# Joints and merge steps in another order, and the rotary exchange of rows by small DMAs instead of a matmul

## The reference

```python
x = layer_norm(ALPHA * x + 0.5 * swiglu_1(x))
xp, q, k, v, xq, gates = split(x @ w_in)      # pool input, attention, cross query, 3 gates of 1024
q, k = rope_partial(q), rope_partial(k)       # first 16 of 64 dims of a head: x1*cos - x2*sin, x2*cos + x1*sin
merged = (sigmoid(g0) * (pool(xp) @ w_br_pool) + sigmoid(g1) * (window_attention(q, k, v) @ w_br_swa)
          + sigmoid(g2) * (cross_attention(xq, mem) @ w_br_cross))
x = layer_norm(ALPHA * x + merged @ w_o)
x = layer_norm(ALPHA * x + 0.5 * swiglu_2(x))  # swiglu: (silu(x @ w_gate) * (x @ w_up)) @ w_down
```

## Time and profile before

| | us |
|---|---|
| median of 3 runs (lowest, highest) | 2549.53 (2546.69, 2554.24) |
| profiled execution | 2552.91 |
| its span, first to last instruction | 2551.1 |
| TensorE busy | 2442.1 (96%) |
| VectorE, ScalarE, GpSimd busy | 64%, 48%, 24% |
| mean granted TensorE clock | 0.982 |

### The profile page before, as it was taken

One profiled execution on the slowest core, in us unless ns is written; L12 is line 12 of the kernel. 1 busy time (PEld: TensorE's weight loads), 2 busy tenths in 40 slices (PEclk: granted clock), 3 DMA queues, 4 the chain that ended last, 5 costly groups with the idle time before them and its releaser, 6 DMA issues.

```text
span 2551.1 us, 45264 instructions
## 1 busy us (share of the span) xinstructions
PE 2442.1 (96%) x17684; PEld 2374.3 (93%) x17684; DVE 1631.7 (64%) x2716; ACT 1221.1 (48%) x2459; POOL 615.6 (24%) x544
## 2 busy tenths in 40 slices
PE   6999999999999999999999999989999999999997
PEld 6999999899999889999989999979999998999996
DVE  2878776435444587777687777664443447878775
ACT  4555555334422365655465556542342225655653
POOL 1333333120000123333323333321100002333332
PEclk9999999989999999999999999989999999999999
DMA  6132223222122212232213222222112222222221
GB/s 222 63 120 83 100 88 122 67 75 56 51 82 75 83 67 100 75 106 86 100 50 110 91 100 88 105 90 94 43 55 75 75 75 83 71 96 100 81 103 54
DMA packets 53523, 220.63 MB, mean 86 GB/s; under 512 B 15520, under 2 KB 18464, under 8 KB 40224
## 3 DMA queue, kind: packets, MB, share of 16 engines
q1 hardware_dynamic: 53312, 217.74, 25.1%
HBM read 213.64 MB, written 6.04 MB: 86 GB/s over the span
## 4 chain that ended last, share of the span: by engine, by line
PE 78%; DVE 12%; ACT 5%; DVEq 2%; issue 2%; DMA 0%; POOL 0%; ACTq 0%
PE pair L1796 12%; PE pair L1798 11%; PE pair L1797 11%; PE pair L1648 9%; PE pair L1650 9%; PE pair L1652 9%; PE S L1734 2%; DVE htl L1104 2%; PE S L1796 2%; PE S L1798 2%; PE S L1797 2%; ACT hth L660 1%; PE S L1890 1%; DVE TP L1024 1%; PE TP L1950 1%
## 5 line engine op out<-in xcount | busy, mean ns | idle before, releaser
L1796 PE MATMUL pair<-xth,hiA 128*128 128x288 f32 x1216 | 358.9, 295 | 13.9 <-ACT c L712 7.8
L1797 PE MATMUL pair<-xtl,hiA 128*128 128x288 f32 x1216 | 358.8, 295 | 0.0
L1798 PE MATMUL pair<-xth,loA 128*128 128x288 f32 x1216 | 358.4, 295 | 0.0
L612 ACT ACTIVATE hiA<-TP 128x512 fp32r<-128x512 f32 (+1 forms) x372 | 194.0, 555 | 220.0 <-DVE TP L1029 136.0
L1562 POOL TENSOR_TENSOR loB<-rawB,hiB 128x512 fp32r<-128x512 f32 (+1 forms) x128 | 159.5, 1247 | 480.2 <-ACT hiB L612 480.2
L1010 DVE TENSOR_TENSOR loA<-rawA,hiA 128x1024 fp32r<-128x1024 f32 x108 | 133.9, 1240 | 218.7 <-ACT hiA L599 218.3
L1648 PE MATMUL pair<-xh,hiA 128*128 128x288 f32 x1088 | 253.8, 310 | 18.9 <-DVE loA L1010 9.0
L1015 DVE TENSOR_TENSOR loA<-TP,hiA 128x512 fp32r<-128x512 f32 (+1 forms) x372 | 236.3, 635 | 31.7 <-ACT hiA L612 29.0
L1650 PE MATMUL pair<-xl,hiA 128*128 128x288 f32 x1088 | 243.0, 300 | 0.0
L1652 PE MATMUL pair<-xh,loA 128*128 128x288 f32 x1088 | 242.7, 300 | 0.0
L1796 PEld LDWEIGHTS pair<-xth,hiA 128*128 128x128 f32 x1216 | 228.0, 187 | 15.4 <-issue 15.3
(11 more groups left out here) (322 smaller groups left out, 7001.2 us busy)
## 6 DMA issues: line engine op xcount, KB each, us to landing
rawA<-in_wblk SPq DMA_DIRECT2D x108, 512.0 KB, 3.5
rawB<-in_wg SPq DMA_DIRECT2D x44, 1024.0 KB, 4.8
rawA<-in_wg SPq DMA_DIRECT2D x44, 1024.0 KB, 4.8
rawB<-in_wd SPq DMA_DIRECT2D x24, 768.0 KB, 4.2
rawA<-in_wd SPq DMA_DIRECT2D x24, 768.0 KB, 4.4
rawA<-in_wt_d SPq DMA_DIRECT2D x4, 1024.0 KB, 4.7
rawB<-in_wt_d SPq DMA_DIRECT2D x4, 1024.0 KB, 4.8
mcs<-in_mks SPq DMA_DIRECT2D x2, 2048.0 KB, 10.0
```

The costliest lines, as they stand in the source:

```text
L612: nc.scalar.activation(slot((hiA, hiB), prod, n), src, ACT.Copy).then_inc(f_hi, 1)
L1796: nc.tensor.matmul(bank, wt_hi, xt[0], start=start, stop=False, skip_group_check=True)
L1797: nc.tensor.matmul(bank, wt_hi, xt[1], start=False, stop=False, skip_group_check=True)
L1798: last = nc.tensor.matmul(bank, wt_lo, xt[0], start=False, stop=i == n - 1, skip_group_check=True)
```

## The change

Six places. (1) Memory stage: odd pairs are rounded to buffers of their own (`mwh`, `mwl`), x is rounded after the first pair, and the waits of `round_w` follow. (2) The head of the FFN: other orders on ScalarE and VectorE; `u2` of unit 3 is copied right after P1. (3) Pairs 3, 6 and 9 get their first two forms rounded apart, in the step after the fourth down unit. (4) First norm: `rest_w` of the second block after tile 5. (5) Rotary: no `rotate`; SP issues four DMAs a tile from `tmp` to `swapped`, two zeroed buffers, and VectorE waits for them. (6) One merge list of twenty; ScalarE, VectorE, TensorE and the weight packing go through it alike (their loops are left out below).

```diff
-MERGE_STEPS = [(3, 0), (0, 4), (1, 4), (3, 1), (2, 4), (0, 5), (3, 4), (1, 5), (2, 5), (3, 5)]
-MERGED = (0, 1, 4, 5, 2, 3, 6, 7)
+MERGE_STEPS = [(3, 0), (0, 4), (1, 4), (3, 1), (2, 4), (0, 5), (3, 4), (1, 5), (2, 5), (3, 2)]
+MERGE_STEPS += [(0, 6), (3, 5), (1, 6), (3, 3), (2, 6), (0, 7), (3, 6), (1, 7), (2, 7), (3, 7)]
+MERGED = tuple(m for what, m in MERGE_STEPS if what == 3)
...
 H_GROUPS = [[(0, 2), (2, 7)] for _ in range(FC // 2)]
-H_GROUPS[3] = H_GROUPS[6] = [(0, 7)]
-H_GROUPS[9], H_GROUPS[10] = [(0, 4)], [(0, 2), (2, 3), (3, 4)]
+H_GROUPS[9], H_GROUPS[10] = [(0, 2), (2, 4)], [(0, 2), (2, 3), (3, 4)]
+PARTED = (6, 12, 18)
...
+        mwh = at("mwh", o_scr, [2, 1024], F32R)
+        mwl = at("mwl", o_ht + 32768, [2, 1024], F32R)
...
+        swapped = [parts["prob1"][:, 0:T], parts["pt"][:, 0:T]]
...
+        def split_of(qq):
+            return (mwh, mwl) if qq < PAIR_MEM and qq % 2 else (wh, wl)
...
+            def load_block(qq, s):
+                b = qq * 2 + s
+                if b >= 2:
+                    sp.wait_ge(w_lo, b - 1)
+                sp.dma_start(raw[:, s, :], wblk[b]).then_inc(raw_in[s], 16)
             def load_pair(qq):
                 for s in range(2):
-                    b = qq * 2 + s
-                    if b >= 2:
-                        sp.wait_ge(w_lo, b - 1)
-                    sp.dma_start(raw[:, s, :], wblk[b]).then_inc(raw_in[s], 16)
+                    load_block(qq, s)
+            def swap_rows(l, i):
+                sp.wait_ge(pair_free[i % 2], n_use(l, Q_IN + i // 2) + 2)
+                if i < 2:
+                    sp.wait_ge(rot_clear, l + 1)
+                else:
+                    sp.wait_ge(rope_done, l * 5 + i - 1)
+                for a in (0, HD):
+                    for to, of in ((a, a + 8), (a + 8, a)):
+                        sp.dma_start(swapped[i % 2][to:to + 8, :], tmp[of:of + 8, i % 2, 0:T]).then_inc(rot_in[i % 2], 16)
...
-                for i in range(2, 6):
-                    load_pair(pq(l, i))
+                for i in range(5):
+                    swap_rows(l, i)
+                    load_block(pq(l, 2 + i // 2), i % 2)
+                load_block(pq(l, 4), 1)
+                load_pair(pq(l, 5))
...
-            def round_w(qq, s, first=False):
+            def round_w(qq, s):
                 act.wait_ge(raw_in[s], (qq + 1) * 16)
-                if not first:
+                if qq > 1 and qq <= PAIR_MEM:
+                    act.wait_ge(blk_done, qq * 2 + s - 3)
+                elif qq > PAIR_MEM:
                     act.wait_ge(blk_done, qq * 2 + s - 1)
-                nc.scalar.activation(wh[:, s, :], raw[:, s, :], ACT.Copy).then_inc(w_hi, 1)
...
-                round_w(0, s, first=True)
-            for l in range(L):
-                for what in range(2):
-                    for s in range(2):
-                        act.wait_ge(blk_done, l * 4 + s + 1 if what == 0 else l * 4 + 4)
-                        n = (2 * what + s) * N_MEM
-                        nc.scalar.activation(mtmp[:, l, n:n + N_MEM], pair[s][:, 0, 0:N_MEM], ACT.Copy).then_inc(pair_free[s], 1)
-                        if l * 2 + what + 1 < PAIR_MEM:
-                            round_w(l * 2 + what + 1, s)
-                    if (l, what) == (1, 0):
-                        act.wait_ge(x_in, 16)
-                        for h in range(2):
-                            for c in range(KC):
-                                nc.scalar.activation(x_form((xth, xbh), h, c), x[:, c, half(h)], ACT.Copy).then_inc(xf_hi, 1)
-                        for q_no in range(4):
-                            fill_head(0, 0, q_no)
+                round_w(0, s)
+            for s in range(2):
+                round_w(1, s)
+            for i in range(PAIR_MEM):
+                for s in range(2):
+                    act.wait_ge(blk_done, 2 * i + s + 1 if i % 2 == 0 else 2 * i + 2)
+                    n = (2 * (i % 2) + s) * N_MEM
+                    nc.scalar.activation(mtmp[:, i // 2, n:n + N_MEM], pair[s][:, 0, 0:N_MEM], ACT.Copy).then_inc(pair_free[s], 1)
+                    if i + 2 < PAIR_MEM:
+                        round_w(i + 2, s)
+                if i == 0:
+                    act.wait_ge(x_in, 16)
+                    for h in range(2):
+                        for c in range(KC):
+                            nc.scalar.activation(x_form((xth, xbh), h, c), x[:, c, half(h)], ACT.Copy).then_inc(xf_hi, 1)
+                if i == 2:
+                    for q_no in range(4):
+                        fill_head(0, 0, q_no)
...
                 fill_head(fb, 2, 3)
                 round_sums(fb, 2)
                 silu(1, 1)
-                round_sums(fb, 3)
-                round_hidden(fb, 0, 0)
-                round_hidden(fb, 0, 1)
-                silu(2, 0)
                 fill_a21(fb, HEADS)
                 fill(fb, HEADS, "P1")
+                round_sums(fb, 3)
                 fill(fb, HEADS, "P5")
+                round_hidden(fb, 0, 0)
+                silu(2, 0)
+                round_hidden(fb, 0, 1)
                 silu(2, 1)
                 fill(fb, HEADS, "P2")
...
+                    def copy_u2():
+                        act.wait_ge(f_done, done(fb, u, "P6"))
+                        if u > HEADS:
+                            act.wait_ge(de_free, unit_count(fb, u - 1))
+                        nc.scalar.activation(u2[:, :], al[u % 2], ACT.Copy).then_inc(al_act, 1)
                     if on:
                         copy_p1(fb, u)
                     if u == HEADS:
-                        round_hidden(fb, 1, 0)
+                        copy_u2()
                     elif on:
...
-                    if g:
-                        act.wait_ge(f_done, done(fb, u, "P6"))
-                        if u > HEADS:
-                            act.wait_ge(de_free, unit_count(fb, u - 1))
-                        nc.scalar.activation(u2[:, :], al[u % 2], ACT.Copy).then_inc(al_act, 1)
+                    if u == HEADS:
+                        round_hidden(fb, 1, 0)
+                    elif g:
+                        copy_u2()
...
-                    elif old and (j_old % 2 or len(groups) > 1):
+                    elif old and (j_old % 2 or j_old not in PARTED):
                         round_hidden(fb, j_old // 2, len(groups) - 1 if j_old % 2 else 0)
+                    elif not old and u > HEADS and SEQ[u - 1][2] == 3:
+                        act.wait_ge(f_done, done(fb, u - 1, "P3"))
+                        round_hidden(fb, SEQ[u - 2 - SEQ[u - 1][2]][1] // 2, 0)
...
                 rest_of_sums(fb, 2)
+                first_sums(fb, HEADS)
                 head_hidden(fb, 1, 1)
                 hidden_sums(fb, 0)
                 hidden_sums(fb, 1)
                 rest_of_sums(fb, 3)
+                rest_of_sum(fb, HEADS, "P5")
+                second_sum(fb, HEADS)
                 rest_of_hidden(fb, 0, 0)
-                rest_of_hidden(fb, 0, 1)
-                first_sums(fb, HEADS)
                 dve.drain()
                 head_hidden(fb, 2, 0)
-                rest_of_sum(fb, HEADS, "P5")
-                second_sum(fb, HEADS)
+                rest_of_hidden(fb, 0, 1)
                 head_hidden(fb, 2, 1)
                 rest_of_sum(fb, HEADS, "P6")
                 third_sum(fb, HEADS)
                 rest_of_sum(fb, HEADS, "P7")
                 hidden_sums(fb, 2)
-                rest_of_hidden(fb, 1, 0)
...
                     if g_old:
                         hidden_sums(fb, j_old)
-                        if j_old % 2 or len(groups) > 1:
+                        if j_old % 2 or j_old not in PARTED:
                             rest_of_hidden(fb, j_old // 2, len(groups) - 1 if j_old % 2 else 0)
+                    elif u == HEADS:
+                        rest_of_hidden(fb, 1, 0)
+                    elif d_old and SEQ[u - 1][2] == 3:
+                        rest_of_hidden(fb, SEQ[u - 2 - SEQ[u - 1][2]][1] // 2, 0)
...
                     if c == 3:
                         rest_w(pq(l, Q_IN), 0)
                         tail_onto_x(fb, 2, 1)
+                    if c == 5:
+                        tail_onto_x(fb, 3, 1)
+                        rest_w(pq(l, Q_IN), 1)
                 rest_of_x(0, KC - 1)
-                tail_onto_x(fb, 3, 1)
-                rest_w(pq(l, Q_IN), 1)
                 tail_into_mean(2, 1)
                 tail_into_mean(3, 1)
...
+                for t in swapped:
+                    last = nc.vector.memset(t, 0.0)
+                last.then_inc(rot_clear, 1)
...
                 def rope(i):
                     dst = q[:, i, :] if i < 4 else k[:, :]
                     dve.drain()
-                    dve.wait_ge(rot_done, l * 5 + i + 1)
+                    dve.wait_ge(pair_free[i % 2], n_use(l, Q_IN + i // 2) + 2)
                     nc.vector.tensor_tensor(dst, tmp[:, i % 2, 0:T], cst[:, C_COS:C_COS + T], ALU.mult)
```

(40 more changed lines are left out.)

146 lines of the change are left out of this document (60 added, 86 removed).

## The result

The changed kernel took 2526.23 us (median of 4 runs, 2525.46 to 2527.96) against 2549.84 for the kernel before in the same runs. The ratio estimated from these runs is 0.9905, with a 95% interval of 0.989 to 0.992. The profiled execution took 2526.76, with a span of 2525.0 against 2551.1: 26.1 us less, where the sum of the prediction was 28.1.

What follows compares the result with a forecast made beforehand. TensorE, busy nearly the whole span with 109 us idle, was taken to bound the kernel. Terms summed to -28.1: 2552.9 profiled to 2524.8, or 2522 against the median; range 2514 to 2530 (0.64), wider 2512 to 2537.

Steps and rivals of the forecast that it cites:

- Head: Head of the FFN: waits move from P1 to P5 and from P7 to P4, a net cost of 3.6 us.
- I take a loss of 0.9: FFN head: P4's start between 0.5 us gained and 1.4 lost; 0.9 lost taken, four times, making +3.6.
- the upper bound of the term: FFN head: +10 us, if the wait at P5, near 3 us, also costs 1.6 of clock.
- rival 2: FFN head costs its upper bound, by the clock: 6.4 us more, 2528; chance 0.09.
- Prologue: Memory stage: with a second set of weight buffers, products wait only for bank copies; gain 4.5 us, bounds 1 and 6.
- Rotary: Rotations by DMA, not matmul: 0.96 us saved for each of eight blocks, landings covered; net gain 7.3 us.
- Rivals 1 and 4: 1: swaps not hidden, rotary's 7.3 gone, 2529, chance 0.12. 4: swaps hold SP's queue and VectorE, 2558, chance 0.04.
- rival 3: Merge: the wait returns at the next merge step, 2531; chance 0.03.
- Merge: Merge steps: a gate block between two merge steps removes a 3.24 us wait and 1.59 of half clock, twice; gain 9.7.
- Hidden: Hidden forms of chunks 6 and 12 rounded apart: 1.08 us off each of eight waits for c; gain 8.6.
- First norm: First norm: earlier rest_w of the second block shortens the 3.71 us wait; 0.8 a layer taken, gain 1.6.
- the bound of 2 a layer: First norm: at most 2 us a layer can reach the second half's chain; between nothing and 2, 0.8 was taken.

Runs made afterwards that it cites:

- head_old: Changed kernel with both lists of the FFN head and the place of the u2 copy as before; span 2519.3 us, ratio 0.9864 to the kernel before.
- late_rest: Changed kernel with VectorE's rounding rest of chunks 0 and 1 moved behind the last head product; span 2514.2 us, ratio 0.9863 to the kernel before.
- best: Changed kernel with prologue bank copies ahead of the next roundings and two VectorE rests behind the last head product; span 2514.7 us, ratio 0.9862.
- swap_8: Changed kernel with each of the four DMAs of a rotary swap cut in two by columns, making eight; span 2525.9 us.
- merge_true: Changed kernel with the merge list of before and the two exceptions at the ends of each half of it; span 2537.2 us.
- parted_old: Changed kernel with the hidden forms of chunks 6 and 12 rounded all at once, as before; span 2528.1 us.

## Why the prediction was right, and where it was not

**Right in what moves, and nearly in the sum, with some luck.** 28.1 were forecast and 26.1 measured, and the median, 2526.2, lies inside the range. But by their own stretches the six edits are worth 23.7, 4.4 less than forecast; the 2.4 that bring it to 26.1 lie mostly behind the last mean, where nothing was edited. Against the median the sum makes 2521.4 (2549.5 less 28.1), not quite the 2522 that I wrote. Of the 4.8 us by which the measured median is above that, 2 are the sum's; the other part is the step from the profiled execution to the median. I took off the 3.4 us by which the execution of before lay above its median, and the one of after lay 0.5 above its own.

**Head: right mechanism, mis-sized, +3.6 against +9.7.** The waits went where the prediction had put them, from P1 to P5 and from P7 to P4. On the time scale of before (the head's last three matmuls began at 927.53 and 913.16, a shift of 14.37) P5 came at 933.4, within the forecast 931.9 to 933.8. Both meetings with GpSimd happened: 1.87 us in place of 0.76 at 914.52, and 1.39 in place of 0.46 at 905.31, together 2.0 us. The failed step is "I take a loss of 0.9", which left out the clock. P4 came 11.0 after P5, not 9.5, as a part of the products behind the 3.19 ran at half clock. Where the clock stayed, in three FFNs of other kernels with the same lists, P4 came 9.49 after P5, so the chain itself was sized right. The 9.7 is the upper bound of the term, and rival 2, in three of four FFNs. I argued against it with waits of up to 2.8 that cost no clock, though the wait that I forecast, near 3, lay nearer to the 3.24 of the earlier trace rows, which did. Nor was the argument safe: in head_old two of the same three waits did cost it, hidden in part by a shorter wait at P7. Of the 9.7, 7.8 lie behind the head's last matmul. 1.0 us in the second FFN and 0.5 in the last lie ahead of it, where the granted clock was lower (0.93 from the first head product on, against 0.97 before), and 0.4 in the third, at full clock in both kernels. head_old and late_rest show the cause; two operations of 1.35 and 1.65 us on VectorE were all that P5 waited for, as best shows.

The Trainium skill, "SBUF — State Buffer", section "Who interferes with whom", has the later of two such operations blocked until the other ends. The trace agrees in the main: VectorE's operation, begun 0.04 us after GpSimd's, ended at 916.39, 0.61 us after GpSimd's end at 915.78, where the whole operation takes 0.76 alone.

**Prologue, -4.5 against -3.7.** The long wait came at 24.39 (24.2 forecast) and for the reason given; the three products after it, with their waits, took 0.1 to 0.4 us more each than I had put.

**Rotary, -7.3 against -7.0.** From the first issue to the use of the data I had put 5.2 us, 1.7 of issues and 3.5 of landing. It was 4.4 in a layer's first swap: the issues took longer, 0.66 to 0.78 us each and not 0.43, and the landing shorter, 1.6 behind the last issue. The cover hid both, and swap_8 shows that there was room. Rivals 1 and 4 fall, and rival 3 with the merge below.

**Merge, -9.7 against -9.9.** The sum was right to the wait and its clock, and merge_true gives it back. But with the old list, dropping the exceptions of the half lists gives half of it by itself; that the same edit also drops them was not seen. Whether the new list alone would give all of it is open.

**Hidden, -8.6 against -9.2,** as argued. **First norm, -1.6 against -3.6** in these two executions, 2.8 by the means: inside the bound of 2 a layer, and the price that I feared, the clock falling there, was paid in 13 of the 24 layers traced.

## What to carry to other kernels

A reordered list moves a wait; what it costs is set by the last operation that the next product needs, and by what stands ahead of that on its engine. Find it by its end time, and move behind it whatever that product does not need, one operation at a time. Read an edit's worth from its own stretch of the timeline, for the span of one execution moved by several microseconds where nothing was edited. And price a wait that you forecast with the clock of the waits nearest to it in length on both sides, not with the harmless ones alone.

## What the runs showed of the hardware

The half clock behind a wait is not settled by the wait. In the nine kernels with the head of the change P5 waited 3.18 to 3.20 us in 26 cases; in 23 of them P4 followed 10.9 to 12.1 us later, in three 9.49. Two windows of parted_old, in which the granted clock, PEclk, stands before the last two numbers:

```profile
1324.40:1329.40 5.00, 4.97 (x37) 5.00 (x38) 2.19 (x4) 1.50 (x4) 0.49 (x1) 1.00 0.00 0
920.00:925.00 5.00, 4.91 (x26) 4.94 (x27) 2.25 (x4) 0.03 (x1) 0.00 (x0) 0.68 0.02 5
```

Both begin behind a wait of 3.19. In the first the clock stays at 2.4 GHz and 37 matmuls fit, in the second it is at 1.2 for a part and 26 do. In best, P6's wait of 1.50 brought 0.54 in one FFN and left two others at full speed; of the waits of 2.5 to 2.8 in the old head none brought it in the kernel before and two of three in head_old (0.66 both times). The Trainium skill, "TensorE: Matmul & The Clock Gate", section "Part 1: The HAM clock gate", says that the gate looks at TensorE's activity in time slots of its own that do not start with the kernel, so that the same kernel differs from run to run. These rows agree in so far as a wait of one length cost the clock in one FFN and not in another; the slots themselves do not show.

Four small DMAs between SBUF tensors, each of 8 rows of 2304 bytes, hold SP's queue for 2.64 to 3.12 us. In the first layer's first swap, where VectorE stood waiting, the data were used 1.6 us after the last issue's end (471.43 less 469.85).
